# Modulation sums by products with a column of ones, and four of them at other places

## What is computed

```
c_silu = jax.nn.silu(c)
mods = jnp.split(c_silu @ ada_w[layer] + ada_b[layer], N_MOD, axis=-1)
shift, scale = jnp.split(c_silu @ kv_ada_w + kv_ada_b, 2, axis=-1)
...
h = modulate(rms_norm(x, norm_g[layer, 0]), sh, sc)     # h * (1 + scale) + shift
x = x + MACARON_WEIGHT * (1.0 + g)[:, None, :] * swiglu(h, ffn_w_in[layer, 0], ffn_w_out[layer, 0])
```

## Time and profile before

| | |
|---|---|
| median of 3 runs | 1209.98 us (1209.83 to 1212.27) |
| time of the profiled execution | 1208.38 us |
| its span, from first to last instruction | 1206.5 us |
| TensorE busy | 1187.9 us |
| VectorE busy | 800.3 us |
| ScalarE, GpSimd busy | 586.7 us, 556.9 us |
| granted TensorE clock over the span | 0.999 |
| moved from and to memory | 297.92 MB, 247 GB/s |

### The profile page before, as it was taken

The page is one execution under the profiler, slowest core; times in us unless marked ns, Lnnn a source line. Parts: engine busy times, 40 slices in busy tenths (PEclk is TensorE's granted clock), DMA queues, the critical chain, the costliest instruction groups (busy, mean ns, idle before and its releaser), DMA issues.

```text
span 1206.5 us, 15432 instructions
## 1 busy us (share of the span) xinstructions
PE 1187.9 (98%) x5752; PEld 975.4 (81%) x5752; DVE 800.3 (66%) x1118; ACT 586.7 (49%) x764; POOL 556.9 (46%) x418
## 2 busy tenths in 40 slices
PE   9999999999899999899999999999999999999998
PEld 6888887887688888788888888888888887888887
DVE  6885468844687688578768666697683675644423
ACT  5566465665543443444434357444352665534440
POOL 1466334564544343555454226764452462445460
PEclk9999999999999999999999999999999999999999
DMA  9976369845698899549988748799884444866550
GB/s 355 356 273 227 108 244 333 287 146 184 215 344 287 304 337 349 168 155 339 302 301 315 279 174 273 250 327 303 303 297 165 150 154 157 261 211 208 209 193 35
DMA packets 183224, 297.92 MB, mean 247 GB/s; under 512 B 8368, under 2 KB 100208, under 8 KB 183152
## 3 DMA queue, kind: packets, MB, share of 16 engines
q1 hardware_dynamic: 177696, 284.82, 68.2%
q10 hardware_dynamic: 5456, 12.13, 2.9%
HBM read 295.84 MB, written 1.08 MB: 246 GB/s over the span
## 4 chain that ended last, share of the span: by engine, by line
PE 88%; DVE 5%; POOL 2%; ACT 2%; issue 1%; SPq 1%; DMA 1%; ACTq 0%; DVEq 0%
PE ps L1821 26%; PE ps L1834 26%; PE ps L1826 25%; PE ps L2087 2%; PE ps L1848 1%; POOL w_lo L510 1%; PE ps L1971 1%; PE ps L1913 1%; PE ps L1999 1%; ACT w_hi L640 1%; DVE w_lo L1157 1%; PE ps L1987 1%; DMA raw<-w_in 1%; SPq L468 1%; PE ps L1959 1%
## 5 line engine op out<-in xcount | busy, mean ns | idle before, releaser
L510 POOL TENSOR_TENSOR w_lo<-raw,w_hi 128x512 fp32r<-128x512 f32 x348 | 479.5, 1411 | 447.0 <-ACT w_hi L640 447.0
L640 ACT ACTIVATE w_hi<-raw 128x2048 fp32r<-128x2048 f32 x188 | 354.6, 1910 | 102.9 <-PE ps L1834 68.8
L1821 PE MATMUL ps<-w_hi,h_hi 128*128 128x512 f32 x1120 | 313.8, 402 | 1.0 <-issue 1.0
L1834 PE MATMUL ps<-w_lo,h_hi 128*128 128x512 f32 x1120 | 301.4, 391 | 2.7 <-POOL w_lo L521 0.8
L1826 PE MATMUL ps<-w_hi,h_lo 128*128 128x512 f32 x1120 | 300.6, 390 | 0.0
L1157 DVE TENSOR_TENSOR w_lo<-raw,w_hi 128x2048 fp32r<-128x2048 f32 x96 | 224.9, 2346 | 111.4 <-ACT w_hi L640 108.6
L1834 PEld LDWEIGHTS ps<-w_lo,h_hi 128*128 128x128 f32 x1120 | 209.3, 188 | 50.1 <-issue 2.1
L1826 PEld LDWEIGHTS ps<-w_hi,h_lo 128*128 128x128 f32 x1120 | 210.1, 188 | 46.2 <-DVE h_lo L1218 0.2
L1821 PEld LDWEIGHTS ps<-w_hi,h_hi 128*128 128x128 f32 x1120 | 200.6, 188 | 43.7 <-issue 6.9
L1143 DVE SCALAR_TENSOR_TENSOR ps<-ada_raw,ccol,ps 128x512 f32<-128x512 f32 x240 | 181.0, 754 | 8.7 <-DMA ada_raw<-ada_w 2.0
L913 ACT ACTIVATE a_hi<-ps 128x512 fp32r<-128x512 f32 x44 | 26.3, 599 | 160.6 <-PE ps L2087 160.6
(11 more groups left out here) (198 smaller groups left out, 981.2 us busy)
## 6 DMA issues: line engine op xcount, KB each, us to landing
raw<-ffn_in SPq DMA_DIRECT2D x176, 512.0 KB, 5.7
ada_raw<-ada_w SPq DMA_DIRECT2D x144, 512.0 KB, 7.2
raw<-ffn_out SPq DMA_DIRECT2D x44, 1024.0 KB, 6.5
raw<-w_in SPq DMA_DIRECT2D x31, 1024.0 KB, 8.6
raw<-w_out SPq DMA_DIRECT2D x8, 1024.0 KB, 6.4
ada_raw<-kv_ada_w SPq DMA_DIRECT2D x16, 512.0 KB, 8.5
raw<-w_kv SPq DMA_DIRECT2D x8, 1024.0 KB, 6.0
bias<-na_bias ACTq DMA_DIRECT2D x16, 256.0 KB, 4.2
```

The lines of the kernel that those rows point to most:

```text
L510: ins = pool.tensor_tensor(w_lo[:, u % RAW, piece], raw[:, u % RAW, piece], w_hi[:, u % RING, piece].bitcast(F32), ALU.subtract)
L640: act.activation(w_hi[:, u % RING, :], raw[:, u % RAW, :], ACT.Copy).then_inc(*S.inc("w_hi_ready", u))
L1821: pe.matmul(bank(b), hi[:, k_in_lhs + k, tok], wh[:, k, c * 512:(c + 1) * 512], start=start and k == 0, stop=False)
L1834: ins = pe.matmul(bank(b), hi[:, k_in_lhs + k, tok], wl[:, k, c * 512:(c + 1) * 512], start=False, stop=stop and k == nk - 1)
```

## The change

Each of the 40 sums over partitions is now four matmuls with `ada_acc` as weights and a column of ones (`ones`, filled once at the start by VectorE) as the moving operand. Each gives one column of 128 finished sums, so that VectorE's reduction of 128 x 512 numbers becomes one addition of 128 x 4, which takes in the bias too. The separate bias addition goes, and the multiplication by 1.0. TensorE waits for `ones_ready` once, before its first product. All sums keep their places in the order but four: those at step 29 of both layers of the first block go to step 31, the one behind unit 43 goes behind unit 45, and the last one before the pooling part (behind unit 68) goes between `pool_product(0, ...)` and `mix_across`.

```diff
-SUM_STEPS = (5, 7, 9, 11, 12, 14, 15, 18, 22, 29)
+SUM_STEPS = (5, 7, 9, 11, 12, 14, 15, 18, 22, 31)
...
-        for a, b, wait in ((*QUIET[0], 3), (*QUIET[1], 1), (("up", 0, 0), ("up", 0, 0), 3)):
+        for a, b, wait in ((*QUIET[0], 3), (*QUIET[1], 1), (("up", 0, 0), ("up", 0, 0), 5)):
...
+    in_pool = max(h for h in sum_unit if sum_unit[h] < first["pool"])
+    sum_unit[in_pool] = first["pool"]
...
             def reduce_vector(v, half):
-                dve.wait_ge(*S.at("ada_sumT_done", v, half))
+                dve.wait_ge(*S.at("ada_sum_done", v, half))
                 b = job_bank["ada", v, half]
-                dve.tensor_reduce(mods[:, v, 4 * half:4 * half + 4], bank(b).rearrange("p (k c) -> p k c", k=4),
-                                  AX.X, ALU.add).then_inc(*S.inc("ada_reduced", v, half))
+                cols = slice(4 * half, 4 * half + 4)
+                dve.tensor_tensor(mods[:, v, cols], bank(b)[:, 0:4], bcols[:, v, cols], ALU.add).then_inc(
+                    *S.inc("ada_reduced", v, half))
...
-                link(dve.tensor_tensor(m, m, bcols[:, v, :], ALU.add))
...
-                    ins = dve.tensor_scalar(m, m, 1.0, None, ALU.mult)
+                    S.same("mod_ready", (v,), "ada_reduced", (v, half))
+                    return
...
                 gate_na(layer)
+                for half in sum_step.get((layer, 31), []):
+                    reduce_vector(*half)
...
             modulate_half(1, 1)
+            reduce_vector(*in_pool)
...
                 for k in range(4):
-                    ins = pe.transpose(bank(b)[:, k * P:(k + 1) * P], ada_acc[:, half, k * P:(k + 1) * P], ident[:])
-                ins.then_inc(*S.inc("ada_sumT_done", v, half))
+                    ins = pe.matmul(bank(b)[:, k:k + 1], ada_acc[:, half, k * P:(k + 1) * P], ones[:], start=True,
+                                    stop=True)
+                ins.then_inc(*S.inc("ada_sum_done", v, half))
...
             pool_product(0, acc_use((("pool",), 0), ("x_ready", "f01", 0)), (0, 1, 2, 3))
+            ada_jobs(u)
             mix_across()
             mix(1)
...
             S.same("unit_used", (u,), "acc_done", (("pool",), NT - 1))
-            ada_jobs(u)
```

More of the change, by code:

```diff
@@ L287, in program @@
         minus_half = sb("minus_half", [P, 2 * NH])
+        ones = sb("ones", [P, 1])
         qk_norm = sb("qk_norm", [P, 2, DH])
@@ L1141, in ada @@
                         if part >= 2:
-                            dve.wait_ge(*S.at("ada_sumT_done", (part - 2) // 2, part % 2))
+                            dve.wait_ge(*S.at("ada_sum_done", (part - 2) // 2, part % 2))
                     ins = dve.scalar_tensor_tensor(out=into, in0=src, scalar=c, in1=acc, op0=ALU.mult, op1=ALU.add)
@@ L1177, in sums @@
                         e = sum_unit.get((v, half), NU)
-                        if e + 4 == u and up_sum(e) is None:
+                        if e + 4 == u and up_sum(e) is None and e != first["pool"]:
                             reduce_vector(v, half)
@@ L1438, in _ @@
             dve.memset(row[:, 0:512], 0.0).then_inc(*S.inc("row_zeroed"))
+            dve.memset(ones[:], 1.0).then_inc(*S.inc("ones_ready"))
             dve.memset(stat[:], 1.0).then_inc(*S.inc("stat_filled"))
@@ L2025, in _ @@
             pe.wait_ge(first_in, N_FIRST)
+            pe.wait_ge(*S.at("ones_ready"))
             for layer in range(DEPTH):
```

## The result

| | before | after |
|---|---|---|
| median of 4 runs, us | 1210.99 (1209.83 to 1212.27) | 1228.55 (1227.65 to 1229.60) |
| profiled execution, us | 1208.38 | 1227.65 |
| span, us | 1206.5 | 1225.8 |

A forecast was written before the change was run, and what follows sets the result against it. TensorE was taken to bound the kernel. 37 dearer sums (+16.65), three hidden sums (-1.35) and the wait at unit 43 (-0.87) gave +14.4 us on 1209.98: 1224.4 us, range 1219.5 to 1229.

The forecast's parts named there:

- What bounds the kernel: Whole kernel: TensorE, busy 1187.9 of 1206.5 us; its added time is paid in full, VectorE's savings win only where TensorE waits.
- A sum costs 8 x 0.112 = 0.90 us: Each new sum on TensorE: 8 pairs of load and matmul at 0.112 us, 0.45 us more than the four transposes.
- The reason given: New sums: a plain fp32 pair with 128 x 128 weights is bound by its load, about 0.112 us, whatever it streams.
- the argument from the loads' durations: TensorE's loads: 192 ns in a plain product against 84 with 8 weight columns; the difference, 108, is the pace.
- The moved sums are hidden, the wait at unit 43 goes, 2.2 us: Four moved sums: three disappear in TensorE's waits, -1.35 us; the wait for `ada_acc` at unit 43 goes, -0.87.
- 0.90 "just" fitted: Second layer's end: a moved sum of 0.90 us fits into TensorE's two waits, 0.96 us together, at no cost.
- VectorE's relief counts nothing: VectorE's reductions, additions and multiplications: 26 us less work, counted as nothing because none of TensorE's waits ends on a reduction.
- the 2 us allowed for: Variant for VectorE's relief: where VectorE is behind, 2 us of TensorE's waits may go, giving 1222.4 us.
- `ones` is one small fill while the first inputs arrive: nothing: Start of the kernel: filling the new tile `ones` was claimed to cost nothing.

The follow-up runs named there:

- the good placement: Kernel before plus one unused tile of 64 bytes where the change put `ones`, nothing else: 1208.38 us beside 1210.27, ratio 0.9986.
- moves_64B: Kernel before with the four moved sums and an unused 64-byte tile at the place of `ones`: 1207.18 us beside 1210.52, ratio 0.9969.
- ones_64B: Changed kernel with `ones` in a tile of 64 bytes, one column used: 1223.08 us beside 1210.52 before, ratio 1.0104.
- plain_128_columns: Kernel before with the moves and 64-byte tile, transposes replaced by plain fp32 products with the identity, reductions kept: 1221.76 us, ratio 1.0091.
- sum_fp32r: Changed kernel with `ada_acc` and ones rounded to fp32r, two columns of ones, 64 bytes of new tiles: 1206.74 us beside 1210.47, ratio 0.9967.

## Why the prediction was right, and which term was missing

**What bounds the kernel**: right. TensorE's added time was paid in full, and 29 us off VectorE brought nothing that a measurement shows. TensorE's busy time rose by 22.4 us, where 15 were forecast: 19.3 us of longer span and 3.1 us less idle time.

**A sum costs 8 x 0.112 = 0.90 us**: right, 0.91 by the trace: unchanged by 128 columns for one, about halved by half the pairs. In device time a sum in the open costs 0.43 us more (15.9 / 37), where 0.45 was forecast and the traces without the clock's stretches give 0.45. The reason given is shown in part. The price goes by pairs and not by moving columns; that it is the load's 128 columns that take the time, and not something fixed in each pair, no run shows, since no pairs with fewer columns of weights stand in a row. And the argument from the loads' durations (192 - 84 = 108, the pace) doesn't hold: a transpose's load lasts 139 ns, by which its pairs should follow each other at 55, but four of them take 0.45 us, 0.11 each. The Trainium skill ("TensorE: Matmul & The Clock Gate", section on LDWEIGHTS) has 107 ns for such a load. The distance of 112 ns from load to load agrees within 5%, the loads' own durations of 139 and 192 ns don't. Its 25 ns from start to start for few columns (section on the back-to-back gap), a formula that by the page leaves the load out, isn't what pairs of load and product show here, at 1, 2 or 128 columns.

**The moved sums are hidden, the wait at unit 43 goes, 2.2 us**: right, 2.3 us by the moves alone. With the dear sums they should be worth 3 x 0.90 + 0.87 = 3.6, and were worth 4.4 by the medians and 3.6 by the starts in the traces. At the second layer's end, where 0.90 "just" fitted, the product starts 0.41 us later than before and the second wait gives 0.45 back.

**VectorE's relief counts nothing**: right; the 2 us allowed for didn't come. The forecast's 774 us of work were 771.2.

**"`ones` is one small fill while the first inputs arrive: nothing"**: this step failed. The fill does cost nothing, but the tile isn't only its fill: it moves the tiles behind it by 32 bytes, and 1044 matmuls that the change doesn't touch run at 233.3 ns in place of 229.1. Measured by itself it is 4.0 us. The three measured terms, 15.9 - 2.3 + 4.0, give the 17.6 us of the result; without the placement it would have been 13.6, close to the 14.4 forecast. That they close to the tenth is luck, since each median can be off by about 1 us: read from traces without the clock's stretches, the terms are 16.6 - 2.2 + 4.2 = 18.6 of the 19.3 us between the spans. That the forecast held is luck in part too. Its range had room for the missing term, with 0.45 us left (1228.55 against 1229).

**Open.** Why the distance matters isn't known: six distances were run, two of them once each, and 128 and 160 weren't among them. The moves (2.3) and the good placement (1.9) together bring 3.3 us, not 4.2; about half of what is missing is the second low stretch of the clock in the trace of `moves_64B`. `ones_64B` is 1.3 us behind `plain_128_columns` though it leaves VectorE less to do. The clock doesn't explain it, since both traces have the same short stretch; in the starts of the two traces it lies in the large products, which neither edit touches. Neither was followed further.

## What to carry to other kernels

Price a small matmul by its pair of load and product where each brings its own weights: count the pairs in the trace, since a plain fp32 product is two, and don't expect fewer columns to make it cheaper. Work taken from an engine that nobody waits for isn't worth time on the one that everybody waits for. A new tile, however small, moves those behind it: when the sum of the known terms doesn't close, compare the untouched matmuls by shape, and try the kernel with the padding alone.

## What the runs showed of the hardware

- Plain fp32 pairs with 128 x 128 weights follow each other at 0.112 us with 1 as with 128 moving columns (median distance of the loads inside a sum, `after` and `plain_128_columns`); pairs of fp32r with 2 columns at 0.111 (`sum_fp32r`; four of them take 0.48 us with what stands at their ends).
- The recorded duration of a load doesn't give the pace: loads of 139 ns (transposes, before) and of 192 ns (plain products, after) start 109 and 112 ns apart.
- The pace of fp32r matmuls of 512 columns depends on the distance between the starts of the stationary and the moving tile modulo 256 bytes: 227 ns at 0, 228 to 230 at 192, 233 at 32, 64 and 224, 234 at 96 (32 and 96 from one run each). In this kernel the spread from best to worst was 6.9 us (1208.38 and 1215.26).
- A stretch of 3.4 us at the lower clock level, some 315 us into the execution, costs this kernel 1.3 to 1.6 us; some executions have it and some don't.
